# Six raw weight buffers whose low part is written in place, and a weight pipeline that stands one tile further ahead

## What is computed

```python
def swiglu(x, w_in, w_out):
    a, gate = jnp.split(x @ w_in, 2, axis=-1)
    return (jax.nn.silu(a) * gate) @ w_out
...
        x = layer_norm(ALPHA * x + 0.5 * swiglu(x, w['ffn_w_in'][l, 0], w['ffn_w_out'][l, 0]), g[0], b[0])
        if l < N_A:
            y, hr, hi = s5_mixer(...)
...
        else:
            y = diff_attention(...)
        x = layer_norm(ALPHA * x + y, g[1], b[1])
        x = layer_norm(ALPHA * x + 0.5 * swiglu(x, w['ffn_w_in'][l, 1], w['ffn_w_out'][l, 1]), g[2], b[2])
```

## Time and profile before

| | us |
|---|---|
| median of three runs | 2319.38 |
| the profiled execution | 2318.73 |
| its span, first to last instruction | 2316.9 |
| TensorE busy | 2257.6 (97%) |
| VectorE busy | 1525.1 (66%) |
| ScalarE busy | 1144.4 (49%) |
| GpSimd busy | 575.2 (25%) |
| mean granted TensorE clock | 0.996 of full speed |

### The profile page before, as it was taken

How to read it: one execution, slowest core, us unless ns; L and a number is a source line. 1 busy time by engine, 2 the same in 40 slices (tenths; PEclk the granted TensorE clock), 3 DMA queues, 4 the chain that set the end, 5 groups by cost and what they waited for, 6 DMA issues and landing times.

```text
span 2316.9 us, 42849 instructions
## 1 busy us (share of the span) xinstructions
PE 2257.6 (97%) x17261; PEld 2217.1 (96%) x17261; DVE 1525.1 (66%) x2292; ACT 1144.4 (49%) x1923; POOL 575.2 (25%) x491
## 2 busy tenths in 40 slices
PE   8989999999998998999999999999999999999999
PEld 8989999999998998999999999999999998999999
DVE  6898768657788578444475575656677665475444
ACT  4434543555645546433365465555466564354332
POOL 2267401123211343111251123010352011132110
PEclk9999999999999999999999999999999999999999
DMA  9568675454765455655569656544556456355452
GB/s 251 168 194 234 191 217 181 123 171 137 218 216 172 138 162 148 183 151 147 151 191 291 189 160 178 154 122 134 148 154 189 135 147 190 115 152 170 143 156 80
DMA packets 705367, 391.15 MB, mean 169 GB/s; under 512 B 25001, under 2 KB 693138, under 8 KB 705170
## 3 DMA queue, kind: packets, MB, share of 16 engines
q1 hardware_dynamic: 662720, 332.44, 49.6%
q10 hardware_dynamic: 42450, 55.96, 7.3%
HBM read 366.53 MB, written 21.82 MB: 168 GB/s over the span
## 4 chain that ended last, share of the span: by engine, by line
PE 75%; DVE 9%; ACT 2%; issue 2%; POOL 1%; ACTq 0%; POOLq 0%; DVEq 0%
PE tile_ps L537 22%; PE tile_ps L539 22%; PE tile_ps L538 22%; DVE wl L515 3%; PE misc L1731 1%; PE misc L1711 1%; ACT wh L509 1%; PE misc L2064 1%; PE misc L2089 1%; POOL zq L870 1%; PE misc L2264 1%; DVE r L828 1%; DVE hs L1539 1%; PE tile_ps L2923 1%; PE misc L1728 1%
## 5 line engine op out<-in xcount | busy, mean ns | idle before, releaser
L515 DVE TENSOR_TENSOR wl<-raw,wh 128x1024 fp32r<-128x1024 f32 (+1 forms) x640 | 796.6, 1245 | 444.2 <-ACT wh L509 442.3
L537 PE MATMUL tile_ps<-xh,wh 128*128 128x256 f32 (+1 forms) x3520 | 1051.9, 299 | 21.4 <-DVE wl L515 16.9
L539 PE MATMUL tile_ps<-xh,wl 128*128 128x256 f32 (+1 forms) x3520 | 1035.5, 294 | 0.0
L538 PE MATMUL tile_ps<-xl,wh 128*128 128x256 f32 (+1 forms) x3520 | 1035.4, 294 | 0.0
L509 ACT CAST wh<-raw 128x1024 fp32r<-128x1024 f32 (+1 forms) x640 | 655.0, 1025 | 734.0 <-PE tile_ps L539 723.3
L537 PEld LDWEIGHTS tile_ps<-xh,wh 128*128 128x128 f32 x3520 | 666.1, 189 | 29.5 <-issue 18.7
L538 PEld LDWEIGHTS tile_ps<-xl,wh 128*128 128x128 f32 x3520 | 666.1, 189 | 0.9
L539 PEld LDWEIGHTS tile_ps<-xh,wl 128*128 128x128 f32 x3520 | 665.9, 189 | 0.0
L725 POOL TENSOR_TENSOR hl<-hf,hh 128x256 fp32r<-128x256 f32 (+1 forms) x176 | 243.7, 1384 | 1269.8 <-ACT hh L633 1269.2
L537 PE MATMUL tile_ps<-hh,wh 128*128 128x320 f32 (+1 forms) x1472 | 441.9, 300 | 5.4 <-DVE wl L515 5.1
L538 PE MATMUL tile_ps<-hl,wh 128*128 128x320 f32 (+1 forms) x1472 | 433.0, 294 | 0.0
(11 more groups left out here) (303 smaller groups left out, 1803.4 us busy)
## 6 DMA issues: line engine op xcount, KB each, us to landing
raw<-in_ffn_w_in_dram SPq DMA_DIRECT2D x352, 512.0 KB, 3.8
raw<-in_ffn_w_out_dram SPq DMA_DIRECT2D x128, 448.0 KB, 3.7
raw<-in_ffn_w_out_dram SPq DMA_DIRECT2D x64, 512.0 KB, 4.0
raw<-in_ssm_w_glu_dram SPq DMA_DIRECT2D x32, 512.0 KB, 3.8
raw<-in_attn_w_kv_dram SPq DMA_DIRECT2D x32, 512.0 KB, 4.0
wt<-scr_w ACTq DMA_DIRECT2D x16, 512.0 KB, 4.7
cp<-scr_c ACTq DMA_DIRECT2D x16, 512.0 KB, 4.3
raw<-in_attn_w_q_dram SPq DMA_DIRECT2D x16, 512.0 KB, 3.9
```

The costliest lines, as they stand in the source:

```text
L515: nc.vector.tensor_tensor(wl[n % WS][:, 0:k, :], raw[n % RAWS][:, 0:k, :], wh[n % WS][:, 0:k, :].bitcast(F32), ALU.subtract).then_inc(w_lo, 1)
L537: nc.tensor.matmul(o, wh[w][:, kk, :], xa, start=kk == 0, stop=False)
L538: nc.tensor.matmul(o, wh[w][:, kk, :], xb, start=False, stop=False)
L539: return nc.tensor.matmul(o, wl[w][:, kk, :], xa, start=False, stop=kk == ROWS[n] - 1)
```

## The change

Six raw buffers take the place of four, and four high buffers the place of three. The three low buffers go: `wl[s]` now names the same bytes as `raw[s]`, and the low part is written over the raw tile. Ten buffers of 4 KB a partition are used before and after. A raw buffer is now busy until TensorE has used the low part in it, so SyncE's wait becomes `tile_done >= n - RAWS + 1` (tile n - 6 finished) in place of `w_lo` (low part of tile n - 4 written). As `WS` is 4, the conversions stand one tile earlier in the programs of ScalarE and VectorE, and the setup converts four tiles instead of three. The 90 matmuls at TensorE's end are taken out.

```diff
-RAWS, WS, PSS = 4, 3, 4
+RAWS, WS, PSS = 6, 4, 4
...
-FILL = ((256, 0, 0), (320, 0, 0), (288, 0, 0), (512, 0, 0), (384, 0, 0), (320, 32, 0), (288, 32, 0), (320, 4, 0), (304, 0, 0),
...
         keep.at += X_LEAD
+        w_at = keep.at
         raw = [keep(f"raw{s}", [P, KMAX, P]) for s in range(RAWS)]
+        low = Map(w_at)
+        wl = [low(f"wl{s}", [P, KMAX, P], F32R) for s in range(RAWS)]
         wh = [keep(f"wh{s}", [P, KMAX, P], F32R) for s in range(WS)]
-        wl = [keep(f"wl{s}", [P, KMAX, P], F32R) for s in range(WS)]
...
         def sp_tile(sp, n, view, col):
-            wait(sp, w_lo, n - RAWS + 1)
+            wait(sp, tile_done, n - RAWS + 1)
             sp.dma_start(raw[n % RAWS][:, 0:ROWS[n], :], view[:, :, col:col + P]).then_inc(w_loaded[n % RAWS], 16)
...
                 dve.wait_ge(w_hi, n + 1)
-                nc.vector.tensor_tensor(wl[n % WS][:, 0:k, :], raw[n % RAWS][:, 0:k, :],
+                nc.vector.tensor_tensor(wl[n % RAWS][:, 0:k, :], raw[n % RAWS][:, 0:k, :],
                                         wh[n % WS][:, 0:k, :].bitcast(F32), ALU.subtract).then_inc(w_lo, 1)
...
-            return nc.tensor.matmul(o, wl[w][:, kk, :], xa, start=False, stop=kk == ROWS[n] - 1)
+            return nc.tensor.matmul(o, wl[n % RAWS][:, kk, :], xa, start=False, stop=kk == ROWS[n] - 1)
...
             dve_lo(dve, 2)
+            dve_lo(dve, 3)
...
             act_hi(act, 2)
+            act_hi(act, 3)
...
-            for cols, at, w_at in FILL:
-                for j in range(5):
-                    w, x = wh[j % 2][:].rearrange("p k c -> p (k c)"), (hh, hl)[j % 2][:].rearrange("p k n -> p (k n)")
-                    nc.tensor.matmul(ps[:, 0, 0:cols], w[:, w_at:w_at + P], x[:, at:at + cols],
-                                     start=True, stop=True, skip_group_check=True)
```

More of the change, by code:

```diff
@@ L131 @@
 BUSY_NORMS = {(0, 1): 10, (2, 1): 5, (3, 1): 4}
-FILL = ((256, 0, 0), (320, 0, 0), (288, 0, 0), (512, 0, 0), (384, 0, 0), (320, 32, 0), (288, 32, 0), (320, 4, 0), (304, 0, 0),
-        (320, 0, 16), (320, 16, 0), (448, 0, 0), (256, 32, 0), (320, 0, 4), (272, 0, 0), (320, 0, 32), (192, 0, 0), (320, 8, 0))
 HID = {}
```

## The result

The changed kernel takes 2336.22 us (median of five runs, 2335.12 to 2336.81) beside 2319.38 us before (five runs, 2317.69 to 2323.73). The ratio is 1.0069, 95% interval 1.0057 to 1.008: 17 us slower. The prediction, 2321 us with a range of 2309 to 2330, was wrong. The profiled execution took 2335.12 us, its span is 2333.3, 16.4 more than before, and its mean granted clock is 0.985 where it was 0.996.

The account below looks back on a forecast made before the run. TensorE was taken as the bound. From the profiled 2318.73 us, -2.2 (lead) + 3.4 (clock) + 1 (loads) + 0 = +2.2 gave 2320.9, stated as 2321 us, range 2309 to 2330.

Parts of the forecast that it names:

- The bound and the place of the gain: TensorE is the bound; the lead gains 2.2 us, at its waits for low parts at 208.80 and 1203.42.
- The closing waits: TensorE's waits for VectorE's result ending a full stretch grow by what it saved; `hs` and `kT` to 3 to 6 us.
- The clock: Term for TensorE dropping to 1.2 GHz behind the gathered waits: +3.4 us, bounds none and 13.6.
- two such falls of 1.7: Two drops of TensorE's clock behind closing waits, ahead of stretches where TensorE is the bound, 1.7 us each: +3.4 us.
- four closing waits: TensorE's waits at 761.75 and 431.07 (`hs`), 926.84 (`kT`) and line 1098, where the short waits would gather.
- my upper bound, 13.6: Most that the clock term could cost TensorE: four falls of 3.4 us.
- The loads: Loads leaving later may hold ScalarE's casts and VectorE behind them: +1 us, bounds 0 and 4.8 for each of two stretches.
- two margins: After a load leaves, TensorE needs the low part 13.7 us later; ScalarE reaches the cast after 5.5 us (median landing 3.8).
- In place 0: Writing VectorE's low part over its input costs zero; bounds no difference, or up to 10 us in the full stretches.
- the 90 matmuls 0: Taking out the matmuls at TensorE's end changes nothing, as the last store lands later: zero, bounds 0 and 1 us.
- one of them, with 0.12: Rival: casts waiting for loads hold gates and scan, 10 us; with four clock falls 17 us: 2336, chance 0.12.
- its clause on the clock: Part of the 2336 rival: TensorE's clock falls at all four closing waits, 4 x 1.7 us.

Follow-up runs that it names:

- e8: The changed kernel with half as many idle matmuls as e5 in each place (8, 4, 6, 7, 15, 8, 7): 2330.44 us, ratio 1.0037.
- e5: The changed kernel with idle TensorE matmuls sized to fill the waits for `hs`, `kT`, one `zq` and two for `r`: 2323.17 us, ratio 1.0008.
- e10: The changed kernel with five raw buffers in place of six, so each load leaves one tile later: 2380.0 us, ratio 1.0255.
- e2: The changed kernel without the one-tile lead (WS back at 3), with six raw buffers and in-place low parts kept: 2320.26 us, ratio 0.9995.
- e1: The changed kernel with the 90 matmuls put back at TensorE's end: 2336.18 us, ratio 1.0064.
- e6: The changed kernel, but from tile 4 on TensorE opens tile n only when low part n + 1 is there: 2324.83 us, ratio 1.0011.
- e7: The kernel before the change, with idle matmuls (5 and 14) in its own two waits for `r`: 2320.38 us, ratio 0.9997.
- e11: The kernel before, with the idle matmuls of e7 and more before waits for `ebuf`, `cp` and `zc`: 2321.52 us, ratio 0.9999.
- e3: The changed kernel with idle matmuls (32, 16, 28, 28, 30) before the waits for `hs`, `kT` and one `zq`: 2330.25 us, ratio 1.0038.

## Why the prediction was wrong

*The bound and the place of the gain: right.* The lead helps only where a low part is late and nothing of VectorE closes the stretch. I named the two places, 208.80 and 1203.42, and 2.2 us; the stretches around them got 1.85 and 1.76 us shorter, which is 1.4 us more than I counted.

*The closing waits: right.* I wrote that "the closing result comes when it came before, and TensorE, early by what it saved, waits for it by so much longer". `hs` came at 431.18 after 431.07, the first `r` at 83.30 after 83.19 (the latter read from the trace of before), low-part waits went from 22.0 to 9.8 us (I said under 10), the longest `hs` and `kT` waits are 4.2 and 3.8 us (I said 3 to 6). VectorE is as full as it was, if the windows are moved along with the work; it has no time to give back (compare). I had also said that the clock would be 1.00 inside these stretches; in one of them it is 0.96:

```profile
405.00:431.00 26.00, 24.21 (x51) 1.00 0.61 185
669.00:706.00 37.00, 35.87 (x73) 1.00 0.66 197
732.00:771.00 39.00, 37.71 (x74) 0.96 0.60 179
```

*The clock: the step that failed.* "I take two such falls of 1.7: +3.4 us. Bounds: none, and four of 3.4 = 13.6." The mechanism was right, its size was not. There are eleven falls with 57.8 us at 1.2 GHz where there were five with 20.4, an increase of up to 18.7 us of work and not 3.4. Three things were wrong in it. First, I counted four closing waits and took two; all four brought a fall, and so did two that weren't on my list, that for `hs` at 705.96 (2.33 us) and that for `zq` of the norm at 593.77 (2.7 us). Secondly, I priced a fall by the mildest rows, 1.7 us; behind three of the four closing waits (3.6 to 4.4 us) the clock is down for 6.8 or 10.2 us, and the stretches of tiles around them got 2.9, 4.7 and 3.1 us longer. Only behind `kT` it is 3.4, and 1.8 us longer. Thirdly, I looked only at the edges of VectorE's full stretches. Three falls came at waits that had hardly changed: 570.8 (`xl`, longest 1.6 before and 1.8 now), 826.8 (`zc`, 1.5 and 1.8) and 1775.7, where the wait of 2.2 us for `ex` is the same in both. The trace of before already held two falls of this kind that I hadn't read, at 229.7 behind 1.74 us (`cp`) and at 751.9 behind 1.97 us (a low part). Even my upper bound, 13.6, would have given 2331, above the range that I set: the range was narrower than the term allowed.

The Trainium skill says of these waits ("TensorE: Matmul & The Clock Gate", section "HAM oscillation — how this bites in real kernels") that one idle gap that is long enough sends the array back to half rate, at a price of half the throttled time. The price agrees roughly: from the end of the wait for `hs` at 431 to the start of tile 116 the changed kernel takes 13.0 us and before took 8.4, so 4.6 us are lost for 10.2 at 1.2 GHz, a little less than half. One gap, one fall, is too simple a picture for this trace: a fall of 10.2 us stood behind a wait of 2.43 us (e8), and one began within a wait of 1.77 that another of 1.08 had preceded (e5).

*The loads: right for this change.* I took +1 us; the closing results came at most 0.3 us later. ScalarE's waits for loads did grow, from 7.2 us, and 1.5 for another group, to 32.8, nearly unfelt. The prediction gave two margins, that of the low part ("13.7 us" against "12.6 and 6.1") and that of the cast, "two tiles or 5.5 us after the load left", and said of the second: "Gates and hidden values queue behind that." e10 shows that the second is the one that counts: with one tile less, 2.75 us, a landing of 3.8 no longer fits. What I expected of e10 rested on the first and missed by 44 us.

*In place 0 and the 90 matmuls 0: right* (1.244 us; e2, e1).

*The rivals.* 2336 was one of them, with 0.12, but for a mechanism of which more than half was late loads. It puts 10 us on late loads, where well under 1 us is seen. The time is right by chance; only its clause on the clock (falls at all four closing waits) holds, and that one with too small a price.

*What stays open.* Which wait brings a fall depends on more than its length. The wait for `ex` was followed by none before and by one after; behind the wait for `hs` at 431, 1.7 to 1.8 us long, before had no fall, and e6, e7 and e11 had one of 6.8 us; the runs of several kernels spread over 6 to 11 us, in e7 with the clock (2317.3 to 2318.5 at 0.996 to 0.998, 2322 to 2325 at 0.993 to 0.994), in e5 not (2319.56 at 0.992, 2325.81 at 0.993). I can't say from these runs which history before a wait decides.

## What to carry to other kernels

Where TensorE is the bound, idle time has a shape as well as a sum: before you let it run further ahead, find what it will wait for at the end of the stretch, since here most waits of 1 to 2 us cost only themselves (not all: 1.7 us before `hs` brought 6.8 us at 1.2 GHz in e7 and e11), and one of about 4 us cost 1.5 to 4.6 us more behind it. But ask of a fall, too, what TensorE waits for next: that at 124 us cost nothing. Fill such a wait with idle matmuls of measured size (the full size gave back 13 us, half of it 6, and twice as much, in five of the seven places, no more than 6), and then read the granted clock again, as the next wait may take its place. When you shorten a ring of buffers (here the raw ones, used in turn), ask of the first engine that touches the load what else stands in its queue, and not only when the consumer at the end is starved.

## What the hardware showed that I had not expected

- The row of a slow stretch reads like that of a fast one: 7.00 of 7.00 us busy, with 36 matmuls instead of 60 and a clock of 0.51 instead of 1.00. A tile's matmul of 256 columns starts every 0.213 us there instead of every 0.117.
- Behind a 2.43 us wait the clock was down for as long (10.2 us) as behind one of 4.24.
- A fall of the clock can cost nothing: without that of 6.8 us at 124, TensorE arrived 2.7 us early and waited 2.82 us for `ebuf` (e7).
- An idle matmul of 128 x 128 float32 runs as two passes of 0.12 us each (60 passes in 6.86 us), which made e3's filling twice too long.
- A ring one buffer shorter (five for six) took 1.9%, with loads that land as fast as before (median 3.8 us, longest 8.6 in both).
